# RWKV scan of a two-part block network: who copies the output sums, who subtracts the means, where the key steps, the second quad and the constants' loads stand

## The reference, cut to what matters

```python
kk = (k * k_k).reshape(B, S, H, N);  kk = kk / jnp.maximum(jnp.linalg.norm(kk, axis=-1, keepdims=True), 1e-12)
k = k * (1.0 + (a - 1.0) * k_a)
def step(state, inp):
    r_t, w_t, k_t, v_t, kk_t, a_t = inp
    sk = jnp.einsum('bhvk,bhk->bhv', state, kk_t)
    state = state * w_t[:, :, None, :] - sk[..., None] * (kk_t * a_t)[:, :, None, :] + v_t[..., None] * k_t[:, :, None, :]
    return state, jnp.einsum('bhvk,bhk->bhv', state, r_t)
_, ys = lax.scan(step, s0, ...)
y = head_norm(y, LNX_EPS) * lnx_g + lnx_b
bonus = jnp.sum(rh * kh * r_k, axis=-1, keepdims=True) * vh
out = jnp.einsum('bsf,fd->bsd', (y + bonus) * jax.nn.silu(g), w_out)
```

## Time and profile before

| | us |
|---|---|
| median of three runs | 4136.34 |
| lowest and highest run | 4133.54, 4146.91 |
| the profiled execution | 4140.06 |
| its span, first to last instruction | 4138.2 |
| PE busy in the span | 3889.8 (94%) |
| DVE, ACT, POOL busy | 1698.1, 1201.9, 673.4 |
| mean granted TensorE clock | 0.978 |

### The profile page before, as it was taken

How to read it: one execution, slowest core, us unless ns; L and a number is a source line. 1 busy time by engine, 2 the same in 40 slices (tenths; PEclk the granted TensorE clock), 3 DMA queues, 4 the chain that set the end, 5 groups by cost and what they waited for, 6 DMA issues and landing times. The chain is left out here.

```text
span 4138.2 us, 70086 instructions
## 1 busy us (share of the span) xinstructions
PE 3889.8 (94%) x29746; PEld 2318.9 (56%) x29746; DVE 1698.1 (41%) x3599; ACT 1201.9 (29%) x2182; POOL 673.4 (16%) x389
## 2 busy tenths in 40 slices
PE   8999999989989999999998998997999978888898
PEld 3458844445456666644554446444544467888643
DVE  3346621133134444431332008225544457565422
ACT  1147720012246656511221009112200212222114
POOL 0000000000000000142000000332122137574442
PEclk9999999999999999999999999998999999999999
DMA  6000042131221011111102000101232221212301
GB/s 224 21 21 2 2 163 82 51 89 72 107 85 65 24 47 24 64 49 56 47 16 102 16 31 11 67 35 34 82 130 84 77 91 48 69 44 80 118 5 41
DMA packets 173323, 256.14 MB, mean 62 GB/s; under 512 B 50532, under 2 KB 96084, under 8 KB 173014
## 3 DMA queue, kind: packets, MB, share of 16 engines
q1 hardware_dynamic: 173016, 251.67, 17.7%
HBM read 189.33 MB, written 62.05 MB: 61 GB/s over the span
## 5 line engine op out<-in xcount | busy, mean ns | idle before, releaser
L1180 POOL TENSOR_TENSOR lg_seven_s<-other_columns 128x512 f32<-128x512 f32 x4 | 5.1, 1267 | 1760.7 <-POOLq L112 1740.2
L2060 DVE TENSOR_SCALAR_CACHE_REDUCE la_s<-psum 128x512 f32<-128x512 f32 (+1 forms) x384 | 210.3, 598 | 190.9 <-PE psum L2126 190.9
L2033 ACT ACTIVATE la_pT<-psum 128x512 f32<-128x512 f32 x320 | 173.0, 593 | 217.6 <-PE psum L2136 217.6
L2024 ACT ACTIVATE la_s<-la_s,la_negm 128x1280 f32<-128x1280 f32 x128 | 174.6, 1364 | 17.5 <-DVE la_negm L2069 13.8
L286 PE MATMUL psum<-room,columns 128*128 128x512 f32 x400 | 173.4, 592 | 0.8 <-DMA room<-in_even_w_in_dram 0.8
L2136 PE MATMUL psum<-ident,la_s 128*128 128x128 f32 x1280 | 166.2, 277 | 0.1
L2136 PEld LDWEIGHTS psum<-ident,la_s 128*128 128x128 f32 x1280 | 138.9, 140 | 41.1 <-issue 35.7
L4126 PE MATMUL psum<-rs_inverse,rs_Z 64*64 64x64 f32 x2560 | 155.3, 221 | 1.6 <-issue 0.3
L2120 PE MATMUL psum<-la_kT,la_qT 64*128 64x512 f32 (+1 forms) x672 | 143.0, 544 | 7.5 <-DVE la_s L2060 7.5
L4124 PE MATMUL psum<-rs_Z,rs_inverse 64*64 64x64 f32 x2048 | 134.3, 223 | 16.5 <-DVE rs_Z L3979 15.8
L286 PE MATMUL psum<-first_weights,columns 128*128 128x512 f32 x288 | 134.8, 623 | 15.3 <-PEq L112 15.3
(11 more groups left out here) (635 smaller groups left out, 7947.5 us busy)
## 6 DMA issues: line engine op xcount, KB each, us to landing
later_slots<-in_ada_w_dram SPq DMA_DIRECT2D x16, 1024.0 KB
rwkv_raw<-x_rows SPq DMA_DIRECT2D x64, 256.0 KB, 2.0
room<-rwkv_raw SPq DMA_DIRECT2D x32, 512.0 KB, 4.3
room<-in_even_w_in_dram SPq DMA_DIRECT2D x6, 2048.0 KB, 11.3
room<-in_odd_w_in_dram SPq DMA_DIRECT2D x6, 2048.0 KB, 12.8
ada_slots<-in_ada_w_dram SPq DMA_DIRECT2D x8, 1024.0 KB, 10.3
rwkv_raw<-room SPq DMA_DIRECT2D x16, 512.0 KB, 2.6
latent_v<-lp_v SPq DMA_DIRECT2D x10, 512.0 KB, 2.6
```

The lines of the kernel that those rows point to most:

```text
L2024: act.activation(s_sb[:, g % 2, j, :], s_sb[:, g % 2, j, :], ACT.Exp, bias=negm[:, g % 2, j:j + 1], accum_out=total[:, g % 2, j:j + 1]).th ...
L2033: act.activation(pT[:, h, at * BANK:(at + 1) * BANK], pT_banks[turn], ACT.Copy).then_inc(pT_moved[turn], 1)
L2060: dve.tensor_scalar(s_sb[:, g % 2, j, cols], s_banks[j][:, 0:cols.stop - cols.start], SCALE, NEG, ALU.mult, ALU.max, accum_out=smax[:, g % ...
```

## The change

- **Output sums.** DVE's `deviations` is gone. ScalarE copies Y from banks 6 and 7 to `dev` (`move_output`, new semaphore `y_moved`), and `lower` waits for that copy. DVE sums `dev` behind unit 0 of the next tile (`output_sums`). GpSimd subtracts the means (`deviations`), behind the first level.
- **Masks and quads.** DVE runs the four `mask_quad` in a row. PE runs quads 0 and 1 of the next tile ahead of `within`, 2 and 3 behind it.
- **Key steps.** GpSimd's `keys` keeps two steps; the other two (`rest_of_keys`) wait for the first level of the tile.
- **Sums in the inverse loop.** `variances` goes from behind unit 1 to behind unit 7, `bonus_sums` from 10 to 14.
- **ScalarE's order.** `move_output` first, then `less_one`, `move_started`, `square_keys`, `means`, `decays`, `norm_keys`, `own_decays`, `square_deviations`, `norm_heads`.
- **Constants in two sets.** Six small tables on `params_in`, issued first; values 0, keys 1, the gain rows and, on `late_in`, the two `lnx` rows behind them, for which only GpSimd waits. PE waits for `params_in` only ahead of `chunk_decays(0)`.

```diff
-        KEY_CONSTS, CONSTS = 6, 8
+        KEY_CONSTS, TABLES, LATE_CONSTS = 6, 6, 2
-        DECAYS_FROM, VAR_AT, NORM_AT, BONUS_AT = 0, 1, 2, 10
+        DECAYS_FROM, SUM_AT, NORM_AT, VAR_AT, BONUS_AT = 0, 0, 2, 7, 14
             eng.tensor_tensor(t1, t1, k_a, ALU.mult).then_inc(q["key_steps"], 1)
+
+        def rest_of_keys(eng, i):
+
+            s = i % 2
+            eng.wait_ge(q["first_steps"], i * FIRST_STEPS)
             eng.wait_ge(q["key_steps"], i * KEY_STEPS + 1)
...
-                scan.sp_gains(sp, (k_k, k_a, r_k))
...
-                                 (levels[:, :, :], a["levels"]), (lnx_g[:, :], param("rwkv_lnx_gain_2")), (lnx_b, param("rwkv_lnx_bias_2"))):
+                                 (levels[:, :, :], a["levels"])):
                     sp.dma_start(dst, src).then_inc(q["params_in"], 16)
                 load_values(0)
+                load_keys(1)
+                scan.sp_gains(sp, (k_k, k_a, r_k))
+                for dst, src in ((lnx_g[:, :], param("rwkv_lnx_gain_2")), (lnx_b, param("rwkv_lnx_bias_2"))):
+                    sp.dma_start(dst, src).then_inc(q["late_in"], 16)
                 load_gates(0)
-                load_keys(1)
                 load_values(1)
...
-                pool.wait_ge(q["params_in"], CONSTS * 16)
+                pool.wait_ge(q["late_in"], LATE_CONSTS * 16)
...
+                def deviations(i):
+                    pool.wait_ge(q["mean_made"], i + 1)
+                    tt(heads(dev[:, :]), heads(dev[:, :]), fan(mean[:, :], N), ALU.subtract).then_inc(q["dev_made"], 1)
+
                 for i in range(NT):
                     if i + 1 < NT:
                         keys(pool, i + 1)
+                        rest_of_keys(pool, i + 1)
                     if i:
                         pool.wait_ge(q["first_steps"], (i + 1) * FIRST_STEPS)
+                        deviations(i - 1)
                         start_output(i - 1)
...
+                def move_output(i):
+                    act.wait_ge(q["y_prod"], i + 1)
+                    if i:
+                        act.wait_ge(q["y_steps"], i * Y_STEPS)
+                    copy(pairs(heads(dev[:, :])), apart(core.banks(6, 2))).then_inc(q["y_moved"], 1)
...
-                def deviations(i):
-
-                    dve.wait_ge(q["y_prod"], i + 1)
-                    Y = apart(core.banks(6, 2))
-                    dve.tensor_reduce(mean[:, :].rearrange("p (n e) -> p n e", e=2), Y, AX.X, ALU.add).then_inc(q["summed"], 1)
-                    if i + 1 < NT:
-                        mask_quad(i + 1, 1)
-                    dve.wait_ge(q["mean_made"], i + 1)
+                def output_sums(i):
+                    dve.wait_ge(q["y_moved"], i + 1)
                     if i:
-                        dve.wait_ge(q["y_steps"], (i - 1) * Y_STEPS + 3)
-                    tt(pairs(heads(dev[:, :])), Y, pairs(fan(mean[:, :], N)), ALU.subtract).then_inc(q["dev_made"], 1)
+                        dve.wait_ge(q["dev_made"], i)
+                    dve.tensor_reduce(mean[:, :], heads(dev[:, :]), AX.X, ALU.add).then_inc(q["summed"], 1)
...
                 def lower(i):
                     if i:
                         pe.wait_ge(q["s_moved"], i * CHUNKS + 1)
-                        pe.wait_ge(q["dev_made"], i)
+                        pe.wait_ge(q["y_moved"], i)
...
-                pe.wait_ge(q["params_in"], CONSTS * 16)
                 for n in range(ITEMS):
                     turn_rows(0, n)
+                pe.wait_ge(q["params_in"], TABLES * 16)
                 chunk_decays(0)
...
-                        quad(i + 1, 0)
+                        for n in range(2):
+                            quad(i + 1, n)
                     within(i)
                     if ahead:
-                        for n in range(1, QUADS):
+                        for n in range(2, QUADS):
```

More of the change, by code:

```diff
@@ L3899, in _ @@
                     if i:
-                        means(i - 1)
+                        move_output(i - 1)
                     if i + 1 < NT:
@@ L4004, in _ @@
                 dve.memset(S[:, :, :], 0.0).then_inc(q["s_moved"], 1)
-                dve.wait_ge(q["params_in"], CONSTS * 16)
+                dve.wait_ge(q["params_in"], TABLES * 16)
                 for n in range(QUADS):
@@ L4024, in _ @@
                     if i + 1 < NT:
-                        mask_quad(i + 1, 0)
-                        deviations(i)
-                        for n in range(2, QUADS):
+                        for n in range(QUADS):
                             mask_quad(i + 1, n)
```

23 lines of the change are left out of this document (13 added, 10 removed).

## The result

The changed kernel takes 4113.96 us, the median of five runs (4113.28 to 4119.23). The kernel before, run beside it on the same chip, takes 4144.95 us (4133.54 to 4147.89). The ratio is 0.994, with a 95% interval from 0.9927 to 0.9953, so it is faster by 0.5 to 0.7%, some 25 us. The two medians by themselves lie 31.0 us apart, but before's five runs spread over 14 us, and a second comparison, with 17 runs of before, gave 0.9942; so I go by the ratio. The forecast was 4106, with a range from 4092 to 4123. The time lies in it, 8 us above the forecast.

The account below looks back on a forecast made before the run. PE's work was taken to bound the scan (477.55 of 560.30 us), leaving only its waits, some 83 us, to win. -12 - 19.8 - 3 + 4.8 = -30; 4140.06 - 30 - 3.7 gave about 4106, range 4092 to 4123.

Parts of the forecast that it names:

- start: Scan's beginning: PE starts without waiting for constants, first quad 10.4 us earlier; 12 us won, bounds 7 and 15.
- change of tile: PE's waits between tiles: 2.5 us won at each of two changes, 3.2 at four, 2 at the last; 19.8 in all.
- clock: Behind four changes of tile: shorter PE waits avoid some falls to 1.2 GHz; 3 us won, bounds 0 to 7.
- inverse loop: Units of the inverse: moved sums and the `max` waiting under GpSimd's deviations cost PE 4.8 us, bounds 0 and 12.
- covered: GpSimd's chain behind the first level: 6.7 us longer, cover falls from 15 to 8 us, at no cost.
- the 1 to 3 us for the key steps: Tile 0's first level: its second half is clear because `rest_of_keys` waits for it, adding 1 to 3 us.
- four overlapped key steps turning into two: Later changes of tile: fewer GpSimd key steps over DVE's first level; 0.6 to 0.7 us more won per change.
- the one on the first level: Change from tile 1 to 2: DVE's L3966 waits for `keys`' first step, L3973 for the second, to about 3486.4.
- The sum behind unit 0: Inverse loop: DVE's 1.2 us output sum is mostly hidden, since PE's `decays` lets DVE catch up; costs 0.15 us.
- The 0.4 behind unit 7: Inverse loop: the moved variance sum costs PE a new gap of 0.4 us there, as before behind unit 1.
- The case in which the `max` waits out a whole step of 2.4 us: Inverse loop, six tiles: the `max` waits 2.4 us instead of 1.4, the time 6 us higher, 4112.
- only one DVE instruction of the kind that overlaps is left: In the loop: argument against the rival that GpSimd becomes the bound (chance 0.04, 4155 us).

Follow-up runs that it names:

- the second pair of traces: The kernel before and the changed kernel, each run once more unchanged for another trace: 4128.28 us (single execution) and 4115.59 us (ratio 0.9942).
- The output part alone: Changed kernel without the constants part and the key steps' wait, leaving ScalarE's copy, GpSimd's deviations, masks, second quad, sums' places: 4136.26 us, ratio 0.9987 to before.
- gated kernel: Changed kernel with GpSimd's last output step (times the gates) waiting until the tile's second state step is done: 4111.96 us.

## Why the prediction was right, and where it was not

The sum was -30; the profiled pair gave -20.8, the ratio -25 (0.6% of 4140). By its terms:

| term | said | measured in the profiled pair |
|---|---|---|
| start | -12 | -9.8, and the stage began 1.2 sooner |
| change of tile | -19.8 | -16.7 |
| clock | -3 | not won; low clock 44.5 to 49.9 us |
| inverse loop | +4.8 | +0.9 |
| covered | 0 | +6.4 |

**Start: right in size, and in the larger of its parts.** PE's first turned item (3326 said, 3324.57 measured) and its first quad (3335.2 said, 3333.1 measured) came as placed; from the stage's start the quad came 11.3 us sooner, where I had 10.4. The piece up to `decays` got 9.8 us shorter, and 12.5 in the second pair of traces. The constants alone shorten it by 12 in both of their traces. What failed is the 1 to 3 us for the key steps: alone they shorten the piece by 4 to 5 us, but on top of the constants by nothing (26.0 without them, 27.9 and 25.7 with). PE's lead met two "issue" waits, 4.35 us together, and a GpSimd that began its key steps at 3342.63, as late as before (3343.24), because its condition was now a load behind all the first tile's, so that L3685 fell on the first level's L3987 (2.87 us).

**Change of tile: nearly right in size, wrong in its cause.** I built the 2.5 to 3.2 us out of DVE's reduction and deviations, 2.45 us, "gone from it", and priced four overlapped key steps turning into two at 0.6 to 0.7. The output part alone gave next to nothing at the changes (128.3 against 129.4 and 123.2). The key steps alone came to 115.2, which is 8 to 14 us less, and after's two traces to 112.7 and 110.6. PE's waits at all seven changes show it with less scatter: 35.6 and 33.3 us in before's two traces, 20.1 with the key steps alone, 20.4 and 21.6 in after's. The step that failed is the one on the first level: I let L3966 wait for the first key step and L3973 for the second. In before's trace, from tile 1 to 2, it is the third, L3687, that lies over L3973 (3485.81 to 3488.49, against L3973's 3486.98 to 3489.58), and the fourth over the second half's L3966, which took 1.63 us. These are just the two that the change moves:

```profile
3485.81 2.68 POOL L3687 TENSOR_TENSOR first_weights<-first_weights,room 128x1024 f32<-128x1024 f32 x1
```

```profile
3486.20 0.74 DVE L3969 TENSOR_TENSOR rs_inverse<-psum,rs_first_level 128x256 f32<-128x256 f32 x2
3490.70 1.63 DVE L3966 TENSOR_TENSOR rs_inverse<-rs_A,rs_first_level 128x512 f32<-128x512 f32 x1
```

I had the row that shows L3973 at 2.60 us, but not L3687's, and placed the collision by reckoning. (The quad ahead of `within`, 32 passes at L4098's pace, is 1.04 us and not the 0.9 that I wrote; nothing hangs on it.)

**Clock: not shown.** PE's waits at the changes fell from 36 to 20 us (33 to 22 in the second traces), and the low clock did not fall with them. Two executions of one kernel differ by 9 us (before) and 16 us (after), so a term of 3 us can't be seen in single traces. Nor did the fall that follows the state product's wait come of that wait. Changed and gated kernel, columns as in the earlier trace rows:

```profile
3512.00:3528.00 16.00, 14.01 (x332) 13.41 (x326) 5.72 (x4) 6.30 (x11) 10.27 (x5) 1.00 0.21 69
3528.00:3536.00 8.00, 8.00 (x173) 8.00 (x175) 3.82 (x6) 0.17 (x1) 0.00 (x0) 0.57 0.70 203
```

```profile
3514.00:3530.00 16.00, 15.66 (x353) 14.98 (x355) 3.82 (x4) 6.47 (x11) 7.07 (x3) 0.97 0.23 70
3528.00:3536.00 8.00, 8.00 (x161) 7.98 (x162) 3.53 (x6) 0.18 (x1) 0.00 (x0) 0.57 0.78 239
```

The grant is 0.57 from 3528 to 3536 in both, though PE had been busy for 15.66 of 16 us in the second.

**Inverse loop: the mechanism right, the size too large.** The `max` waits 1.35 us under the deviations (1.4 said), and PE's wait is 1.85 (2.0 said). PE stood 13.1 and 12.2 us at the `max` over seven tiles in after's two traces, against 10.2 and 11.1 in before's, so 1 to 3 us were lost there. It takes the held key steps and the deviations on GpSimd together: with the key steps alone it is 10.7 us, and with their wait undone 8.6. The sum behind unit 0 did hide. The 0.4 behind unit 7 is there (0.47), in place of the 0.39 behind unit 1. The case in which the `max` waits out a whole step of 2.4 us did not come: its longest took 1.88 us.

**Covered, for nothing: this is the step that failed.** I saw that the finish ends 7 us later, and asked only whether SP's queue is held. It isn't. But DVE's `state` runs there, and `S * eC` reads two operands from SBUF. I had written that in the loop only one DVE instruction of the kind that overlaps is left, and had looked for it in the units alone. The piece from `weigh` to the state grew by 6.4 us, and by 6.9 in the second pair of traces. The gated kernel shows that 3 to 6 of them are this step's: with that one step moved the product is at 0.69 us everywhere, and its piece of the tile at 122.9 us in place of 128.5 and 125.6.

The Trainium skill (SBUF — State Buffer, section Who interferes with whom) says that the ports which DVE and GpSimd share are an exclusive lock, and that a DVE instruction of two SBUF inputs contends with a GpSimd one that reads SBUF. The trace agrees: in tile 2 L4015 ended 0.55 us behind L3812, little less than the 0.69 us that it takes by itself, while L3969 in the kernel before, with one operand in PSUM, took its 0.74 us under GpSimd's L3687.

So the sum promised 9 us more than the profiled pair gave, by terms of both signs: 6.4 missed, 3 for the clock unfounded, 3 too many at the changes and 2 at the start, less 4 too many in the loop and 1.2 that the earlier start of the stage gave for nothing. The median came out 8 us above the forecast. The range held it, with some luck in how the terms offset each other; and since single traces of one kernel differ by 3 to 6 us in such pieces, the smaller of these shares are not shown one by one.

## What to carry to other kernels

Where two engines hold each other up, list every pair of instructions that can meet, with start and end of both from the trace, before and after each moved block. One wait that takes two GpSimd steps off DVE's critical steps gave 17 us by itself; taking 2.4 us of DVE's own work away gave 4 by itself and 1 on top of that wait, because DVE then ran into the GpSimd steps that were left. Parts that add up once need not add up in pairs, so undo each part as well as running it alone. Count a stage's pieces from its own start. A step that moves later for free needs its new neighbours looked up on all engines, and a gate in a loop needs its last pass looked at by itself.

## What the runs showed of the hardware

- When PE starts at once and doesn't first stand 17 to 18 us for the loads, it meets waits without a releaser in the same two places of the first tile, in all nine traces of kernels with early constants: 1.4 to 2.4 us in the quads and 0.5 to 3.0 in `started`. None of the five with the long wait has one there. What makes these waits no run shows.
- GpSimd pays for a collision too: L3690 took 3.15 us in place of 2.36, and L3685 3.34 in tile 0 of the changed kernel's start.
- Without the `max`, seven 16-column instructions of 0.17 us when undisturbed, PE's loop is 11 us shorter (203.8 to 192.5).
